# Pads that bring the weights and all moving operands of the split products to one place modulo 512 bytes

## The reference, cut to what matters

```python
def first_block(...):
    u = rms_norm(x, ln1[i]) * (1.0 + scale1) + shift1
    mix = mixer_sublayer(u, w_in[i], ...)            # proj = u @ w_in, scan, @ w_ssm_out, @ w_o
    x = x + gate1 * mix
    u2 = rms_norm(x, ln2[i]) * (1.0 + scale2) + shift2
    hid = jnp.square(jax.nn.relu(u2 @ w_up[i]))
    x = x + gate2 * (hid @ w_down[i])
    return rms_norm(x, final_norm)

def second_block(...):
    x = x + 0.5 * swiglu(rmsnorm(x, g_ffn1[l]), w1_gate[l], w1_up[l], w1_down[l])
    h = rmsnorm(x, g_mix[l])
    p = h @ w_in[l]
    ...
    x = x + jnp.concatenate([out_a, out_b], axis=-1) @ w_out[l]
    x = x + 0.5 * swiglu(rmsnorm(x, g_ffn2[l]), w2_gate[l], w2_up[l], w2_down[l])
    return rmsnorm(x, g_final)
```

## Time and profile before

| what | value |
|---|---|
| time, median of 3 runs | 2295.98 us (2295.76 to 2298.33) |
| span of the profiled execution | 2287.7 us, 28544 instructions |
| what lies around the span | 8.3 us, from the two above |
| TensorE matmul busy | 2237.3 us, 98%, 10872 matmuls |
| TensorE weight load busy (beside the matmuls) | 1829.0 us, 80% |
| VectorE busy | 1320.4 us, 58% |
| ScalarE busy | 863.7 us, 38% |
| DMA | 222.08 MB, mean 97 GB/s |
| granted TensorE clock, mean | 0.993 |

### The profile page before, as it was taken

How to read it: one execution, slowest core, us unless ns; L and a number is a source line. 1 busy time by engine, 2 the same in 40 slices (tenths; PEclk the granted TensorE clock), 3 DMA queues, 4 the chain that set the end, 5 groups by cost and what they waited for, 6 DMA issues and landing times.

```text
span 2287.7 us, 28544 instructions
## 1 busy us (share of the span) xinstructions
PE 2237.3 (98%) x10872; PEld 1829.0 (80%) x10872; DVE 1320.4 (58%) x1835; ACT 863.7 (38%) x1223; POOL 4.5 (0%) x8
## 2 busy tenths in 40 slices
PE   7999999999999999999999999999989899999998
PEld 5888888887888888888878888889868667888887
DVE  5577777777673475433475344355777766434344
ACT  5655555543222342322342222234445444212124
POOL 0000000000000000000000000000000000000000
PEclk9999999999999999999999999999999899999999
DMA  7323233224543243323222222223121002232321
GB/s 263 114 75 105 96 98 104 92 74 162 169 154 103 92 129 115 101 90 99 92 92 92 92 92 93 92 92 91 49 65 38 19 32 79 92 97 96 103 83 65
DMA packets 208140, 222.08 MB, mean 97 GB/s; under 512 B 9413, under 2 KB 200330, under 8 KB 205994
## 3 DMA queue, kind: packets, MB, share of 16 engines
q1 hardware_dynamic: 206362, 210.26, 28.5%
q10 hardware_dynamic: 1680, 10.49, 1.1%
HBM read 218.57 MB, written 2.16 MB: 96 GB/s over the span
## 4 chain that ended last, share of the span: by engine, by line
PE 87%; DVE 7%; ACT 3%; issue 2%; DMA 1%; ACTq 0%; DVEq 0%
PE G L551 24%; PE G L552 24%; PE G L553 24%; PE G L587 2%; PE G L589 2%; PE G L588 2%; DVE wlo L1806 1%; PE X L739 1%; ACT whi L1159 1%; PE G L1024 1%; DMA araw<-in_w_ada 1%; PE X L1041 1%; PE X L1007 1%; PE X L1031 1%; DVE score L2688 1%
## 5 line engine op out<-in xcount | busy, mean ns | idle before, releaser
L551 PE MATMUL G<-ahi,whi 128*128 128x512 f32 x1496 | 603.0, 403 | 4.1 <-DVE alo L2782 1.4
L552 PE MATMUL G<-alo,whi 128*128 128x512 f32 x1496 | 592.2, 396 | 0.0
L553 PE MATMUL G<-ahi,wlo 128*128 128x512 f32 x1496 | 591.9, 396 | 0.0
L1806 DVE TENSOR_TENSOR wlo<-raw,whi 128x2048 fp32r<-128x2048 f32 x176 | 403.3, 2292 | 240.2 <-ACT whi L1159 236.9
L1159 ACT ACTIVATE whi<-raw 128x2048 fp32r<-128x2048 f32 x176 | 335.5, 1907 | 454.9 <-PE G L553 434.3
L551 PEld LDWEIGHTS G<-ahi,whi 128*128 128x128 f32 x1496 | 282.9, 189 | 72.3 <-issue 2.4
L553 PEld LDWEIGHTS G<-ahi,wlo 128*128 128x128 f32 x1496 | 282.6, 189 | 67.2
L552 PEld LDWEIGHTS G<-alo,whi 128*128 128x128 f32 x1496 | 282.9, 189 | 66.7 <-issue 2.2
L551 PE MATMUL G<-hhi,whi 128*128 128x512 f32 x784 | 310.2, 396 | 0.7 <-DVE wlo L1806 0.7
L552 PE MATMUL G<-hlo,whi 128*128 128x512 f32 x784 | 309.6, 395 | 0.0
L553 PE MATMUL G<-hhi,wlo 128*128 128x512 f32 x784 | 309.5, 395 | 0.0
(11 more groups left out here) (410 smaller groups left out, 2783.6 us busy)
## 6 DMA issues: line engine op xcount, KB each, us to landing
raw<-in_w_in SPq DMA_DIRECT2D x43, 1024.0 KB, 5.1
raw<-in_w_up SPq DMA_DIRECT2D x38, 1024.0 KB, 5.3
raw<-in_w_down SPq DMA_DIRECT2D x32, 1024.0 KB, 5.1
raw<-in_w_gate SPq DMA_DIRECT2D x22, 1024.0 KB, 5.1
braw<-in_w_ada SPq DMA_DIRECT2D x12, 1024.0 KB, 5.1
raw<-in_w_in SPq DMA_DIRECT2D x20, 512.0 KB, 4.5
araw<-in_w_ada ACTq DMA_DIRECT2D x8, 1024.0 KB, 17.7
bc<-acum_dram SPq DMA_DIRECT2D x8, 1024.0 KB, 6.9
```

The source lines that it names most:

```text
L551: pe.matmul(bank[:], wh[:, j, f], rh[:, j, :], start=(j == 0), stop=False)
L552: pe.matmul(bank[:], wh[:, j, f], rl[:, j, :], start=False, stop=False)
L553: last = pe.matmul(bank[:], wl[:, j, f], rh[:, j, :], start=False, stop=(j == k - 1))
L1806: tt(wlo[s][:], raw[s][:], r32(whi[s][:]), ALU.subtract).then_inc(lo_split, 1)
```

## The change

Three things about places in memory, and nothing else: no instruction is added, removed or moved. A tensor `to_weights` of 32 words (128 bytes) is put behind the fixed ones. A place of 112 words (448 bytes) is put behind `pre` in the stage of the scan. The pads of 12 words in the stages `_c` and `_m` get 124 words. Sizes are rounded up to 32 bytes, so the 12 words took 64 bytes and the 124 words take 512.

```diff
-PAD = 12
+PAD = 124
+TO_WEIGHTS, TO_LINE = 32, 112
...
+        fixed("to_weights", [P, TO_WEIGHTS])
         split_a = (("ahi", [P, KB, T], F32R), ("alo", [P, KB, T], F32R))
...
-        (pacc, pre, cv, xf, zs, xdt, xw, btok, sm, seg, bc, states, yf, yhi, ylo, dts, dtw) = after_a(
-            "_s", ("pacc", [P, KB, T]), ("pre", [P, 4, 3 + T]), ("cv", [P, 4, T]), ("xf", [P, 4, T]),
+        (pacc, pre, _, cv, xf, zs, xdt, xw, btok, sm, seg, bc, states, yf, yhi, ylo, dts, dtw) = after_a(
+            "_s", ("pacc", [P, KB, T]), ("pre", [P, 4, 3 + T]), ("to_line", [P, TO_LINE]), ("cv", [P, 4, T]), ("xf", [P, 4, T]),
```

## The result

The changed kernel takes 2252.18 us (median of 4 runs, 2251.57 to 2253.64) against 2295.87 us for the kernel before on the same occasion: a ratio of 0.9817, 95% interval 0.9802 to 0.9832, or 43.7 us less. The forecast was 2264 us, with eight chances in ten for 2235 to 2322 us.

What follows compares the result with a forecast made beforehand. The prediction took TensorE, 98% busy, and the start-to-start distance of 7512 512-column matmuls as the bound; -29 us from these and -3 us from 256-column ones took 2295.98 to 2264 us, eight in ten for 2235 to 2322 us.

Steps and rivals of the forecast that it cites:

- 229.0 ns, the value of chi and clo: Distance of 512-column matmuls before the change, carried over to all 7512: -3.8 ns each, -29 us.
- the rival "the same": 512-column matmuls keep their own rhythm whatever the address difference; unequal hi and lo made chi/clo quick; 2293 to 2300 us, chance 0.27.
- yhi's 233.3 ns at 64 bytes: Counter-evidence in the prediction: yhi and ylo, also 64 bytes from the weights, were not quick, at 233.3 ns.
- -2.3 ns each (-3 us): The 1200 256-column matmuls: half of the gain from 118.3 towards 113.7 ns, -3 us.
- The 8.3 us "around the span": Profiled span 2287.7 us against median 2295.98 us; the difference was said to lie around the span and stay.
- The lower end of the bounds: Ten plain fp32 matmuls at 446 ns, halved to 223 ns a streaming: -74 us on the 512-column matmuls.
- what I costed at nothing: ScalarE writes (at most 3 ns by place), transfers into raw and braw (5.1 us), waits, issue and queues: no change.
- Slower: Rival: at difference 0 weight load and stream collide in all 7512 matmuls; 2323 us in the middle, up to 2350; chance 0.27.
- two reads that can't disturb each other: Skill page's rule against the forecast: separate SBUF read ports for TensorE, so the address difference is worth nothing.

Runs made afterwards that it cites:

- bench_pairs: Separate program, not the kernel: split product's hi, lo, hi order at 16 x 16 places, weights at 0; 226.7 ns lowest, 241.2 highest per 512-column matmul.
- bench_phase: Separate program, not the kernel: streams and weights alternating between place 0 and 64, 128 or 240, 226.7 to 240.2 ns; plain fp32 records 429.2 ns.
- bench_d: Separate program, nothing else at work: 48 float32r matmuls at each of 32 streaming places; 226.7 to 236.7 ns for 512 columns, 113.3 to 120.0 for 256.
- bench_width: Separate program, not the kernel: 128 to 32 weight columns loaded, 226.7 to 233.5 ns at 512 columns streamed; also 448, 384 and 320 columns streamed.
- best: Against the changed kernel, weights used in 256-column matmuls placed 64 bytes further on: 2252.94 us against 2252.99 us on the same chip.

## Why the prediction was right, and where it was not

**Right: what bounds the kernel, and the sum's form.** The gain is in the distance of 512-column matmuls, times 7512. Measured in the stretches: 232.8 - 226.7 = 6.1 ns, and 6.1 x 7512 = 46 us; by the means over the whole traces, 232.8 - 227.0 = 5.8 ns, 44 us. The medians show 43.7 us, the two traces 37.9. The equality of 44 and 43.7 is partly chance, since the executions also differ by the clock.

**Mis-sized: the distance itself.** I took 229.0 ns, the value of chi and clo, as "the row that is nearest to the changed state in the sense that its hi is nearest to the weights". It was 226.7 ns, so the term was 3.8 ns where 6.1 (5.8 over all) were to be had, -29 us for -44 to -46 us. The nearness that I argued from doesn't exist: at 16, 32 and 240 bytes the distance is 231.6, 233.3 and 236.7 ns. The forecast's direction rested on a row that was quick for another reason, the unequal places of hi and lo, which was the argument of the rival "the same". bench_pairs shows that argument right about the row (228.9 for that pair, 232.9 and 233.3 for equal ones) and wrong about the change, since it said a rhythm comes "whatever the difference". I had held yhi's 233.3 ns at 64 bytes against the forecast; it should have weighed more, and the forecast stood on less than I gave it. That the direction came out right was, by this, luck: nothing in the rows said that equal places are good.

**Wrong: the 256-column tiles.** I gave them -2.3 ns each (-3 us); ahi against whi got 1.7 ns slower, and the token-major stage lost 1.2 us. I reasoned from ahi against xwhi, which stood 64 bytes apart, and then brought these to one place as well, so the change took away what I had counted on. Those 19 matmuls were also a good moment of theirs: later in the same trace ahi against xwhi goes at 117.8 ns, hardly quicker than the 118.3 against whi.

**Misread, without effect on the 2264 us.** The 8.3 us "around the span" is the difference of two executions. In one and the same execution it is 1.8 us (2251.57 us, span 2249.8); the profiled execution of before was quicker than the median by the rest. The lower end of the bounds took the ten fp32 records at their common length divided by ten, 446 ns; the distance of such records is 429 ns (bench_phase), and half of it 215 ns, so that bound should have been lower, and it bounds nothing, as float32r stays at 226.7. And 2296 - 53 - 6 gives 2237 us, where the range says 2235.

**Right: what I costed at nothing.** ScalarE's parts take 632 (ahi) and 631 ns (yhi) now that both are at one place, against the earlier trace rows. braw lands after 5.3 us, now at 128, raw at 5.1: 0.2 us that nobody waits for, against the earlier trace rows. VectorE's busy time is the same to 2 us.

**The rivals.** *Slower* by a collision at difference 0 did not come, but its mechanism of one bad place exists: 240 would give 236.7 ns, and 160 made the kernel slower than before. *The same* is refuted by the 6.1 ns. Of two reads that can't disturb each other: the earlier trace rows spoke against it, and so does bench_d. With no other engine and no transfer at work, the same matmuls take 226.7 or 236.7 ns by the place alone. The Trainium skill, page "SBUF — State Buffer", section "SBUF: two separate sides", gives the stream and the weight load ports of their own. The inference that addresses are then worth nothing is what the measurement refutes; whether the loss arises at the ports no run shows. The 216 ns of the Trainium skill's page "TensorE: Matmul & The Clock Gate", section "Back-to-back issue gap", for an isolated gap, were reached at no place: the lowest is 226.7.

**Left open.** How the loss comes about. Shown is that it needs no other engine and no transfer, depends on places modulo 256 bytes, on the columns streamed and loaded and on what went before, and that plain fp32 of the same size doesn't have it. A collision of two reads fits that, but bench_width and bench_phase refute both simple forms of it, and no run here looks inside. I have no rule that foretells the table.

## What to carry to other kernels

Where a kernel is a long run of float32r matmuls, read the distance of their starts, not their duration, and compare stretches with different operands: a few per cent between them are a matter of addresses, and a pad of some words is all it takes. Place streams of 512 columns and their weights at one place modulo 256 bytes, but measure: 160 bytes more made this kernel slower than before the change, and for 448 columns the one place was the worst. For 256 columns 64 bytes apart were best in the sweep (113.3 ns), but in the kernel they mostly gave 117.8 ns and no time. Where TensorE has pauses, expect less: the attention and the out projection took 245 us or more with the quicker matmuls, against 242.9 us before.

## What the runs showed of the hardware that I had not expected

- A period of 256 bytes, with the same 16 values again, for 512 columns to 0.01 ns.
- The lowest distance of float32r matmuls was N + 32 cycles at 2.4 GHz for four widths: 544 for 512 columns (226.7 ns), 480 for 448 (200.0), 416 for 384 (173.3), 352 for 320 (146.7; one place had 146.6). For 256 columns it was N + 16: 272 cycles, 113.3 ns.
- The best place for 512 columns (0: 226.7 ns) is one of the worst for 256 (120.0 against 113.3 at 64).
- At one place two lasting rhythms are possible: 232.4 and 233.3 ns in the kernel before, 236.7 and 233.3 at place 240 in two sweeps, 113.3 and 117.8 ns for 256 columns 64 bytes apart in `best`.
- A plain fp32 matmul of 512 columns is two records of 429.2 ns each, at all four places tried: 858 ns against 226.7 for float32r.
